# Streaming the weights instead of the activations in two weight-heavy products of a two-block transformer kernel

## The chip, the cores and the metric

The kernel runs on one core of a Trainium2 chip. The metric is device time in microseconds (us) for one execution. The program is one launch; the weights come from device memory in 404 blocks of 128 x 1024 float32 numbers (512 KB), used in a fixed order.

Names of the engines in the profile: PE is TensorE's matmul, PEld its load of a stationary operand, DVE is VectorE, ACT ScalarE, POOL GpSimd, SP the engine whose queue issues the block loads.

## The reference, cut to what matters

Two transformer blocks over 256 tokens of width 1024. The change touches one product of each:

```python
def chunk(xc):                                   # first block, expert layer, 16384 experts
    ...
    u_sel = jnp.take(u, experts, axis=0)
    act = gelu(einsum('cd,chkd->chk', xc, u_sel))
    v_sel = jnp.take(v, experts, axis=0)
    return einsum('chk,chkd->cd', (g * act), v_sel)

def conv_ffn(h, w_up, conv_w, conv_b, w_down):   # second block
    u = causal_dwconv(h @ w_up, conv_w, conv_b)
    a, g = jnp.split(u, 2, axis=-1)
    return (silu(a) * g) @ w_down                # w_down: 2752 x 1024
```

The kernel does not gather experts. It keeps a dense routing matrix G (tokens by experts), computes every expert's activation 128 experts at a time, multiplies by G, and multiplies by all rows of `v`: 128 products of (256 tokens x 128 experts) by (128 experts x 1024). The down projection is 22 such products. Each adds into the same 1024 x 256 sum.

## The kernel before, in words

**High and low parts.** A product in float32 precision is made of three in the format fp32r: high weights by high activations, high weights by low activations, low weights by high activations. For each block, ACT writes the high part `w_hi` (L588), then DVE (L1042) or POOL (L487) writes the low part `w_lo = raw - w_hi`. Between block 109 and the end, POOL owns the even blocks (and block 109), DVE the odd ones (`lo_owner`). The rings `raw`, `w_hi`, `w_lo` have four places: ACT may convert block n when PE has finished block n-4 (semaphore `block_used`).

**Two kinds of block.** `project` (L1642) multiplies a block by 1024-wide tokens into one PSUM bank, 24 matmuls, 256 columns moving. `expand` (L2019) takes 128 activations per token from `h_op` (high and low part, two buffers) and adds a 1024 x 256 result into PSUM banks 4 to 7 over all calls, also 24 matmuls: the weight tile of 128 x 128 is stationary, the 256 tokens move. It is called 150 times.

**The stages that call it.** The order within each engine is written out by hand.

- V stage: 64 `expand` blocks in a row. For each, DVE multiplies the stored activation by G (L1383), casts the high part (L1390), subtracts for the low part (L1392; together `split`), and after every other one makes a `w_lo` (L1042). POOL makes the `w_lo` between.
- Chunk stage: 64 times `project` (next 128 experts), ACT's gelu (L888), `split`, `expand`. Per pair of blocks ACT converts two, POOL and DVE make one `w_lo` each.
- FFN stage: 22 tiles, each of two `project` (both halves of the up projection) and one `expand`. DVE adds the earlier token to the PSUM sum (L1565, twice), does four taps of the convolution (L1574) after ACT's first tap (L997), and the gate (L1585, L1590, L1592). Tiles alternate in how many `w_lo` fall to DVE and to POOL: three each in two tiles.

**After the last `expand`** of the V and chunk sum, `add_sum` (L1441) adds the four banks to the residual `res`, ACT and DVE make the operands of the next projection (L621, L1073), ACT squares `res` for the norm, and PE sums the squares (L1657). After the last `expand` of the FFN, the same add leads to the final norm and the output.

Of the kernel before, what the change touches and what calls it, by code (L numbers as in the profile page):

```python
# [29 lines left out]
ALU = mybir.AluOpType  # L30
ACT = mybir.ActivationFunctionType
AX = mybir.AxisListType

P = 128
D = 1024
KT = D // P
NQ = 256
# [23 lines left out]
FT = -(-FF // P)  # L61
# [10 lines left out]
B_IN2 = B_PEER + 2 * (NKEYS - EARLY)  # L72
# [4 lines left out]
N_BLOCKS = B_FFN + 3 * FT  # L77
# [58 lines left out]
def build(nc, dram):  # L136
    ctx = ExitStack()
    with ctx:
# [5 lines left out]
        def sem(name):  # L144
            if name not in sems:
                sems[name] = ctx.enter_context(nc.semaphore(name))
            return sems[name]
# [3 lines left out]
        w_hi = sb("w_hi", [P, RING, D], F32R)  # L151
        w_lo = sb("w_lo", [P, RING, D], F32R)
# [10 lines left out]
        h_op = sb("h_op", [P, 2, 2, NQ], F32R)  # L163
        big = sb("big", [P, NKEYS * NQ])

        ps = ctx.enter_context(nc.psum_tensor("ps", [P, 8, 512], F32))
# [15 lines left out]
        xf = area(KT * NK)  # L182
# [127 lines left out]
        ident = con("ident")  # L310
# [24 lines left out]
        M_IN2 = M_PEER  # L335
# [3 lines left out]
        M_FFN = M_XO + 2  # L339
# [43 lines left out]
        def outputs_read(o):  # L383

            return min(o - 1, HEADS) if o <= HEADS + DH else o - 1

        def walk(a, b):

# [192 lines left out]
        def _(act):  # L581
# [10 lines left out]
            def his(upto):  # L592
                while ahead[0] < min(upto, N_BLOCKS):
                    if lo_owner(ahead[0]):
                        hi(At(ahead[0]))
                    ahead[0] += 1
# [126 lines left out]
            for h in range(DH):  # L723
                for t in range(2):
                    start = FAR - N_META - P * t
# [181 lines left out]
            act.dma_start(w_gate, dram["w_gate"]).then_inc(sem("cst2_loaded"), 16)  # L907
            act.dma_start(flat2(kv_x), mem_store).then_inc(sem("kv_back"), 16)

            def residual_squares(r):  # L910

                for b in range(4):
                    act.wait_ge(sem("res_ready"), 4 * r + b + 1)
                    squares(flat2(res[:, 2 * b:2 * b + 2, :]), 2 * b, NQ, 2)

            his(B_IN2 + 2)
            act.wait_ge(sem("block_used"), B_IN2 - 2)
            for b in range(4):
                act.wait_ge(sem("res_ready"), b + 1)
# [18 lines left out]
            for n in range(NCH):  # L938
                last = csum[:, CHUNK * n + CHUNK - 1:CHUNK * n + CHUNK]
# [60 lines left out]
            def silu(p):  # L1000

                act.wait_ge(sem("conv_done"), p.value(2 * p.first + 1, 2 * p.stride))
                act.activation(act_a[:, p.mod(2), :], conv_a[:, p.mod(2), :], ACT.Silu).then_inc(sem("silu_done"), 1)
# [13 lines left out]
                    tile(At(1 + j, i, 4))  # L1017
            taps(At(FT - 1))
            silu(At(FT - 1))
            residual_squares(1)  # L1020
            root(R_FINAL, NQ)
            for f in range(2):
# [7 lines left out]
        def _(dve):  # L1030
# [401 lines left out]

            def add_sum(r):

                for b in range(4):
                    if b < 3:
                        dve.wait_ge(sem("sum_ready"), 3 * r + b + 1)
                    else:
                        dve.wait_ge(sem("block_used"), (B_IN2, N_BLOCKS)[r])
                    two = flat2(res[:, 2 * b:2 * b + 2, :])  # L1440
                    dve.tensor_tensor(two, ps[:, 4 + b, :], two, ALU.add).then_inc(sem("res_ready"), 1)  # L1441
                    if r == 0 and b:
                        gained_lo(R_MIX, "mix", range(2 * b - 2, 2 * b))

# [26 lines left out]
            for n in range(NCH):  # L1471
                c = slice(CHUNK * n, CHUNK * n + CHUNK)
# [46 lines left out]
            for t in range(2):  # L1519
                w = [pcol("scw", 3 * t + j) for j in range(3)]  # L1520
# [102 lines left out]
        def _(pe):  # L1623
            def parts(s, wa, wb, k_hi, k_lo):

                return ((w_hi[:, s, wa:wb], k_hi), (w_hi[:, s, wa:wb], k_lo), (w_lo[:, s, wa:wb], k_hi))
# [34 lines left out]
            def norm(r, T, bank=2):  # L1661
                for k in range(KT):
                    norm_sum(r, k, T, bank)
# [116 lines left out]
            for h in range(HEADS):  # L1780
                mm = pe.matmul(ps[0:8, 3, 0:NK], one_in[0:NOPE, 7 - h:15 - h], sq[0:NOPE, h * NK:(h + 1) * NK],
                               start=False, stop=(h == HEADS - 1))
# [199 lines left out]
            last = B_BESIDE - B_EARLY - 1  # L1982
# [29 lines left out]
            def expand(n, b, first, last):  # L2012

                s = n.mod(RING)
                for k in range(KT):
                    out = ps[:, 4 + k // 2, (k % 2) * NQ:(k % 2 + 1) * NQ]
                    for j, (w, x) in enumerate(parts(s, P * k, P * k + P, h_op[:, b, 0, :], h_op[:, b, 1, :])):

                        mm = pe.matmul(out, w, x, start=(first and j == 0 and k % 2 == 0), stop=(last and j == 2),  # L2019
                                       skip_group_check=True)  # L2020
                    if last and k % 2 and k < KT - 1:
                        mm.then_inc(sem("sum_ready"), 1)
                mm.then_inc(sem("block_used"), 1)

            def early(c):
                n = At(B_V + c.first, c.i, c.stride)
# [26 lines left out]
            arrived(At(B_IN2 - 1))  # L2053
            pe.wait_ge(sem("acts_ready"), NKEYS)
            expand(At(B_IN2 - 1), (NKEYS - 1) % 2, False, True)

# [125 lines left out]
            def down(p, n, last=False):  # L2184
                arrived(n)
                pe.wait_ge(sem("acts_ready"), p.value(NKEYS + p.first + 1))
                expand(n, p.mod(2), p.first == 0, last)
# [8 lines left out]
            with pe.Fori(0, (FT - 2) // 4) as i:  # L2196
                for j in range(4):
                    tile(At(1 + j, i, 4))
            down(At(FT - 1), At(N_BLOCKS - 1), last=True)
            norm(R_FINAL, NQ)  # L2200


# [138 lines left out]
```

## Time and profile before

| | |
|---|---|
| median of 3 runs | 1556.12 us (1554.26 to 1560.02) |
| profiled execution, first to last instruction (span) | 1548.2 us |
| median less span: start and end around it | 7.9 us |
| PE busy | 1435.7 us (93% of the span) |
| DVE busy | 1175.8 us (76%) |
| ACT busy | 684.5 us (44%) |
| POOL busy | 674.5 us (44%) |
| V stage | 592 to 788 us |
| chunk stage | 788 to 1153 us |
| FFN stage, steady part | 1366 to 1533 us |

The profiled execution has no time of its own beside its span, so the 7.9 us is the difference to the median of the runs. PE's busy share counts overlapping matmuls and does not say that PE is at its peak. An operation that waits for a resource which another engine holds is shown as busy for the whole time, so a long duration of a short operation is a wait.

### The profile page before, as it was taken

To read this page: it belongs to the slowest core of one execution; us is meant where nothing else is said; L and a number is where in the kernel's file an instruction comes from. 1 tells how busy PE (TensorE), PEld (TensorE's weight loads), DVE (VectorE), ACT (ScalarE), POOL (GpSimd) and SP (SyncE) were. 2 spreads that over 40 slices of the span, in tenths; PEclk is the share of its full clock that TensorE was granted. 3 is DMA by queue.
4 is the path that set the end of the run, shared out by engine and by line. 5 is a ranking of instruction groups with operands and counts; after the bars stand their busy time and mean duration, and the time that the engine had idled before them with its cause. 6 is when DMAs were issued, how large, how long until landed. Compare 5 with 4: busy or idle time off the path is not lost.

```text
span 1548.2 us, 31404 instructions
## 1 busy us (share of the span) xinstructions
PE 1435.7 (93%) x11038; PEld 1350.0 (87%) x11038; DVE 1175.8 (76%) x2036; ACT 684.5 (44%) x1035; POOL 674.5 (44%) x300
## 2 busy tenths in 40 slices
PE   7999898998688889899999999999999989899997
PEld 5776588998688889899999999999999968699997
DVE  4424637889899998888878888888875654499997
ACT  4434544444344443333334444444446346555553
POOL 2313246779444443433434444444433335255441
PEclk9999989999799999999999999999999999999999
DMA  7411045666333335666656655565563323255552
GB/s 277 130 55 41 28 139 188 186 196 178 119 116 113 108 114 169 214 213 213 218 169 188 188 179 181 184 189 183 184 211 119 127 96 112 79 183 184 189 176 81
DMA packets 79624, 240.69 MB, mean 155 GB/s; under 512 B 8896, under 2 KB 25552, under 8 KB 78928
## 3 DMA queue, kind: packets, MB, share of 16 engines
q1 hardware_dynamic: 75744, 228.75, 46.2%
q10 hardware_dynamic: 3824, 11.17, 2.0%
q8 instruction: 38, 0.62, 0.2%
q14 instruction: 18, 0.15, 0.0%
HBM read 229.37 MB, written 10.52 MB: 155 GB/s over the span
## 4 chain that ended last, share of the span: by engine, by line
PE 68%; DVE 25%; issue 3%; ACT 1%; DVEq 1%; DMA 0%; POOL 0%; ACTq 0%
PE ps L1642 36%; PE ps L2019 20%; DVE work L1364 6%; DVE work L1383 3%; DVE work L1365 2%; DVE h_op L1390 2%; DVE w_lo L1042 2%; PE ps L1906 2%; PE ps L1860 1%; DVE h_op L1392 1%; PE ps L1657 1%; DVE big L1351 1%; PE ps L1831 1%; DVE big L1349 1%; PE ps L1880 1%
## 5 line engine op out<-in xcount | busy, mean ns | idle before, releaser
L487 POOL TENSOR_TENSOR w_lo<-raw,w_hi 128x1024 fp32r<-128x1024 f32 x241 | 622.0, 2583 | 748.6 <-ACT w_hi L588 748.6
L1642 PE MATMUL ps<-x_op,w_hi 128*128 128x256 f32 (+1 forms) x3968 | 746.7, 289 | 21.1 <-DVE x_op L1060 8.8
L1642 PEld LDWEIGHTS ps<-x_op,w_hi 128*128 128x128 f32 x3968 | 627.8, 194 | 34.3 <-issue 21.2
L1642 PE MATMUL ps<-x_op,w_lo 128*128 128x256 f32 (+1 forms) x1984 | 567.5, 286 | 0.0
L588 ACT ACTIVATE w_hi<-raw 128x1024 fp32r<-128x1024 f32 x400 | 420.5, 1055 | 270.0 <-PE ps L2019 218.2
L2019 PE MATMUL ps<-h_op,w_hi 128*128 128x256 f32 x2400 | 429.3, 280 | 17.1 <-DVE h_op L1392 14.7
L1642 PEld LDWEIGHTS ps<-x_op,w_lo 128*128 128x128 f32 x1984 | 385.7, 194 | 0.0
L2019 PEld LDWEIGHTS ps<-h_op,w_hi 128*128 128x128 f32 x2400 | 367.0, 188 | 19.8 <-DVE h_op L1392 13.6
L2019 PE MATMUL ps<-h_op,w_lo 128*128 128x256 f32 x1200 | 336.2, 280 | 0.0
L1042 DVE TENSOR_TENSOR w_lo<-raw,w_hi 128x1024 fp32r<-128x1024 f32 x159 | 203.7, 1281 | 39.5 <-ACT w_hi L588 39.3
L2019 PEld LDWEIGHTS ps<-h_op,w_lo 128*128 128x128 f32 x1200 | 225.3, 188 | 0.0
L1392 DVE TENSOR_TENSOR h_op<-work,h_op 128x256 fp32r<-128x256 f32 x128 | 194.3, 1518 | 4.4
L1383 DVE TENSOR_TENSOR work<-work,big 128x256 f32<-128x256 f32 x124 | 99.8, 805 | 66.0 <-ACT work L888 65.0
L1364 DVE TENSOR_SCALAR work<-kept,route_t 128x128 f32<-128x128 f32 x256 | 132.8, 519 | 4.7 <-PE ps L2002 2.6
L2002 PE MATMUL ps<-work 128*128 128x128 f32 x512 | 71.2, 283 | 29.3 <-DVE work L1365 29.3
L1365 DVE TENSOR_SCALAR work<-kept,route_t 128x128 f32<-128x128 f32 x256 | 95.4, 373 | 0.0
L2002 PEld LDWEIGHTS ps<-work 128*128 128x128 f32 x512 | 62.9, 193 | 35.2 <-DVE work L1365 35.2
L888 ACT ACTIVATE work<-ps 128x256 f32<-128x256 f32 x64 | 24.7, 386 | 125.0 <-PE ps L1642 125.0
L1390 DVE CAST h_op<-work 128x256 fp32r<-128x256 f32 x128 | 59.4, 464 | 25.7 <-PE ps L2019 14.6
L843 ACT ACTIVATE kv_mem<-ps 128x256 f32<-128x256 f32 x64 | 24.6, 384 | 96.3 <-PE ps L1642 96.3
L868 ACT ACTIVATE big<-ps 128x512 f32 (+1 forms) x64 | 38.2, 598 | 65.3 <-PE ps L2002 65.3
L524 POOL TENSOR_TENSOR big<-big 128x544 f32<-128x544 f32 (+1 forms) x24 | 25.6, 1068 | 81.5 <-DVE big L1229 81.5
(267 smaller groups left out, 1079.4 us busy)
## 6 DMA issues: line engine op xcount, KB each, us to landing
raw<-blocks SPq DMA_DIRECT2D x404, 512.0 KB, 3.4
early_store<-kv_mem SPq DMA_DIRECT2D x60, 128.0 KB, 3.2
work<-early_store SPq DMA_DIRECT2D x60, 128.0 KB, 3.3
big<-consts ACTq DMA_DIRECT2D x2, 1336.0 KB, 6.7
big<-h_t ACTq DMA_DIRECT2D x4, 272.0 KB, 3.9
big<-bias_lines ACTq DMA_DIRECT2D x8, 136.0 KB, 2.6
bias_lines<-route_t ACTq DMA_DIRECT2D x4, 264.0 KB, 3.0
res<-mem_t SPq DMA_DIRECT2D x1, 1024.0 KB, 9.2
```

The source lines that it names most:

```text
L487: pool.tensor_tensor(w_lo[:, s, :], raw[:, s, :], w_hi[:, s, :].bitcast(F32), ALU.subtract).then_inc(sem("lo_pool"), 1)
L588: act.activation(w_hi[:, s, :], raw[:, s, :], ACT.Copy).then_inc(sem("hi_done"), 1)
L868: act.activation(big[:, bass.ds(At(512 * g, i, 4096).value(), 512)], ps[:, 2 + g % 2, :], ACT.Copy).then_inc(sem("g_ready"), 1)
L1042: dve.tensor_tensor(w_lo[:, s, :], raw[:, s, :], w_hi[:, s, :].bitcast(F32), ALU.subtract).then_inc(sem("lo_dve"), 1)
L1364: dve.tensor_scalar(one1[:, g, j, :], con("iota"), route_t[:, 0, tok], None, ALU.is_equal)
L1365: return dve.tensor_scalar(one2[:, g, j, :], con("iota"), route_t[:, 1, tok], route_t[:, 2, tok], ALU.is_equal, ALU.mult)
L1383: dve.tensor_tensor(hf[:, b, :], a, G[:, :, bass.ds(chunk.value(), 1)].rearrange("p t e -> p (t e)"), ALU.mult).then_inc(sem("act_used"), 1)
L1390: dve.tensor_copy(h_op[:, b, 0, :], hf[:, b, :]).then_inc(sem("act_hi"), 1)
L1392: dve.tensor_tensor(h_op[:, b, 1, :], hf[:, b, :], h_op[:, b, 0, :].bitcast(F32), ALU.subtract).then_inc(sem("acts_ready"), 1)
L1642: mm = pe.matmul(ps[:, m_bank, 0:T], w, x, start=(k == 0 and j == 0), stop=(k == last and j == 2))
L2002: mm = pe.matmul(ps[:, 2 + g % 2, P * k:P * k + P], one1[:, g % 2, k, :], one2[:, g % 2, k, :], start=True, stop=True)
L2019: mm = pe.matmul(out, w, x, start=(first and j == 0 and k % 2 == 0), stop=(last and j == 2), skip_group_check=True)
```

## The change: activations stationary, weights moving

In `expand` the roles are exchanged. A tile of activations (128 inner values x 128 tokens) is stationary, and 512 columns of the weight block move. Twelve matmuls of 512 columns take the place of 24 of 256. The sum in banks 4 to 7 now stands with tokens on the partitions, so at the end of each of the two sums it is copied to SBUF (banks in the order of `SUM_ORDER`, ACT the first and third, DVE the second and fourth), transposed by PE in 16 steps into banks 3, 0, 4 and 6, and added to `res` from there.

```diff
+        SUM_ORDER = ((0, 0), (1, 0), (0, 1), (1, 1))
+        sums = xf[:, 0:4 * 512].rearrange("p (j c) -> p j c", j=4)
+        def sum_bank(t, f):
+            return 4 + 2 * t + f
+        def turned_bank(b):
+            return (3, 0, 4, 6)[b]
...
+            def copy_sum(r):
+                for j in (0, 2):
+                    act.wait_ge(*sum_done(r, j))
+                    act.activation(sums[:, j, :], ps[:, sum_bank(*SUM_ORDER[j]), :], ACT.Copy).then_inc(sem("sum_copied_act"), 1)
...
             def add_sum(r):
+                for j in (1, 3):
+                    dve.wait_ge(*sum_done(r, j))
+                    dve.tensor_copy(sums[:, j, :], ps[:, sum_bank(*SUM_ORDER[j]), :]).then_inc(sem("sum_copied_dve"), 1)
                 for b in range(4):
-                    if b < 3:
-                        dve.wait_ge(sem("sum_ready"), 3 * r + b + 1)
-                    else:
-                        dve.wait_ge(sem("block_used"), (B_IN2, N_BLOCKS)[r])
+                    dve.wait_ge(sem("sum_turned"), 4 * r + b + 1)
...
             def expand(n, b, first, last):
                 s = n.mod(RING)
-                for k in range(KT):
-                    out = ps[:, 4 + k // 2, (k % 2) * NQ:(k % 2 + 1) * NQ]
-                    for j, (w, x) in enumerate(parts(s, P * k, P * k + P, h_op[:, b, 0, :], h_op[:, b, 1, :])):
-                        mm = pe.matmul(out, w, x, start=(first and j == 0 and k % 2 == 0), stop=(last and j == 2),
+                for j, (t, f) in enumerate(SUM_ORDER):
+                    out, c = ps[:, sum_bank(t, f), :], slice(P * t, P * t + P)
+                    high, low = h_op[:, b, 0, c], h_op[:, b, 1, c]
+                    w_high, w_low = w_hi[:, s, 512 * f:512 * f + 512], w_lo[:, s, 512 * f:512 * f + 512]
+                    pe.matmul(out, high, w_high, start=first, stop=False)
+                    pe.matmul(out, high, w_low, start=False, stop=False)
+                    mm = pe.matmul(out, low, w_high, start=False, stop=last)
...
+            def turn_sum(r):
+                if r == 1:
+                    pe.wait_ge(sem("bank_free"), M_FFN + 2 * FT)
+                for j, (t, f) in enumerate(SUM_ORDER):
+                    pe.wait_ge(sem("sum_copied_act" if j % 2 == 0 else "sum_copied_dve"), 2 * r + j // 2 + 1)
+                    for k in range(4):
+                        mm = pe.transpose(ps[:, turned_bank(2 * f + k // 2), (k % 2) * NQ + P * t:(k % 2) * NQ + P * t + P],
+                                          sums[:, j, P * k:P * k + P], ident)
+                        if t and k % 2:
+                            mm.then_inc(sem("sum_turned"), 1)
```

On PE, the beginning of one `expand` in the V stage, before. The names are output, moving operand, stationary operand; a row's count is of equal instructions in a row, and `acts_ready` is what `split` signals.

```order
L2019 MATMUL ps<-h_op,w_hi 128x256 [waits acts_ready,lo_pool]
L2019 MATMUL ps<-h_op,w_hi 128x256
L2019 MATMUL ps<-h_op,w_lo 128x256
L2019 MATMUL ps<-h_op,w_hi 128x256 x2
L2019 MATMUL ps<-h_op,w_lo 128x256
```

The same place in the changed kernel:

```order
L2044 MATMUL ps<-w_hi,h_op 128x512 [waits acts_ready,lo_pool]
L2045 MATMUL ps<-w_lo,h_op 128x512
L2046 MATMUL ps<-w_hi,h_op 128x512
L2044 MATMUL ps<-w_hi,h_op 128x512
L2045 MATMUL ps<-w_lo,h_op 128x512
```

The waits stay at the same place; eight such groups of three become four, each of twice the columns.

On PE, from the end of the last `expand` of the V and chunk sum to the next projection (L1642 before, L1667 in the changed kernel), before:

```order
L2019 MATMUL ps<-h_op,w_hi 128x256 x2
L2019 MATMUL ps<-h_op,w_lo 128x256
L1642 MATMUL ps<-x_op,w_hi 128x256 [waits x_even,bank_free,lo_dve]
L1642 MATMUL ps<-x_op,w_hi 128x256
L1642 MATMUL ps<-x_op,w_lo 128x256
```

and in the changed kernel:

```order
L2046 MATMUL ps<-w_hi,h_op 128x512
L2058 MATMUL ps<-kept,big 128x128 [waits sum_copied_act]
L2058 MATMUL ps<-kept,big 128x128 x3
L2058 MATMUL ps<-kept,big 128x128 [waits sum_copied_dve]
L2058 MATMUL ps<-kept,big 128x128 x3
L2058 MATMUL ps<-kept,big 128x128 [waits sum_copied_act]
L2058 MATMUL ps<-kept,big 128x128 x3
L2058 MATMUL ps<-kept,big 128x128 [waits sum_copied_dve]
L2058 MATMUL ps<-kept,big 128x128 x3
L1667 MATMUL ps<-x_op,w_hi 128x256 [waits x_even,bank_free,lo_dve]
```

Sixteen transposes with four waits on copies now stand between the sum and the projection; at the end of the FFN they stand ahead of the final norm's sums.

On DVE, the same place, before (L1042 is the `w_lo` of an odd block, L1073 the low part of the next operand):

```order
L1042 TENSOR_TENSOR w_lo<-raw,w_hi 128x1024 [waits hi_done]
L1441 TENSOR_TENSOR res<-ps,res 128x512 [waits sum_ready] x2
L1073 SCALAR_TENSOR_TENSOR x_op<-res,par,x_op 128x256 [waits rms_hi] x2
L1441 TENSOR_TENSOR res<-ps,res 128x512 [waits sum_ready]
L1073 SCALAR_TENSOR_TENSOR x_op<-res,par,x_op 128x256 [waits rms_hi] x2
```

and in the changed kernel:

```order
L1067 TENSOR_TENSOR w_lo<-raw,w_hi 128x1024 [waits hi_done]
L1462 COPY big<-ps 128x512 [waits sum_ready]
L1462 COPY big<-ps 128x512 [waits block_used]
L1466 TENSOR_TENSOR res<-ps,res 128x512 [waits sum_turned] x2
L1098 SCALAR_TENSOR_TENSOR x_op<-res,par,x_op 128x256 [waits rms_hi] x2
```

Two copies come ahead of the first add, and the second copy waits for the whole sum. Between these places the order of ACT, DVE, POOL and SP is unchanged.

## Rows read from the trace of the kernel before

**Rows 1.** The page: the span.

```profile
span 1548.2 us, 31404 instructions
```

**Rows 2.** Windows by stage: length, busy of PE, PEld, DVE, ACT, POOL; clock, DMA.

```profile
592.00:788.00 196.00, 182.72 (x1537) 180.72 (x1537) 169.09 (x222) 68.33 (x65) 80.39 (x32) 1.00 0.65 208
788.00:1153.00 365.00, 363.62 (x3059) 363.44 (x3058) 291.35 (x255) 150.12 (x189) 153.60 (x63) 1.00 0.59 183
...
1366.00:1533.00 167.00, 166.14 (x1393) 165.97 (x1393) 150.83 (x209) 87.25 (x116) 77.99 (x28) 1.00 0.51 170
```

**Rows 3.** Chain that ended last, chunk stage: start, length, what.

```profile
870.09 2.83 PE ps L2019 x24
...
875.80 2.83 PE ps L2019 x24
```

**Rows 4.** Timeline of DVE, chunk stage: start, length, what, [idle before].

```profile
876.43 0.64 DVE L1383 TENSOR_TENSOR work<-work,big 128x256 f32<-128x256 f32 x1 [0.94 <-ACT work L888]
```

**Rows 5.** Timelines of DVE and POOL, V stage.

```profile
649.05 2.46 POOL L487 TENSOR_TENSOR w_lo<-raw,w_hi 128x1024 fp32r<-128x1024 f32 x1 [2.97 <-ACT w_hi L588]
...
649.33 2.67 DVE L1383 TENSOR_TENSOR work<-work,big 128x256 f32<-128x256 f32 x1
...
652.79 1.22 DVE L1042 TENSOR_TENSOR w_lo<-raw,w_hi 128x1024 fp32r<-128x1024 f32 x1
...
658.97 1.22 DVE L1042 TENSOR_TENSOR w_lo<-raw,w_hi 128x1024 fp32r<-128x1024 f32 x1
...
661.96 2.62 POOL L487 TENSOR_TENSOR w_lo<-raw,w_hi 128x1024 fp32r<-128x1024 f32 x1 [4.92 <-ACT w_hi L588]
...
663.62 1.11 DVE L1390 CAST h_op<-work 128x256 fp32r<-128x256 f32 x1 [1.31 <-PE ps L2019]
```

**Rows 6.** Chain, memory keys: float32 matmuls of 256 columns, stationary 128 x 128.

```profile
140.43 3.46 PE ps L1831 x16
```

**Rows 7.** Timeline of PE: one-column matmuls, and 128 x 128 transposes.

```profile
98.98 1.84 PE L1791 MATMUL ps<-ones,big 96*128 96x1 f32 x16
...
1213.73 1.04 PE L2120 MATMUL ps<-kept,big 128*128 128x128 f32 x8
```

**Rows 8.** Chain, FFN stage.

```profile
1365.90 3.09 PE ps L2019 x24
1368.99 5.74 PE ps L1642 x48
```

**Rows 9.** Timelines of ACT, POOL and DVE, FFN stage.

```profile
1365.42 0.43 DVE L1592 TENSOR_TENSOR h_op<-work,h_op 128x256 fp32r<-128x256 f32 x1
...
1371.89 1.06 ACT L588 ACTIVATE w_hi<-raw 128x1024 fp32r<-128x1024 f32 x1 [1.26 <-PE ps L1642]
...
1373.03 3.49 POOL L487 TENSOR_TENSOR w_lo<-raw,w_hi 128x1024 fp32r<-128x1024 f32 x1 [1.08 <-ACT w_hi L588]
...
1373.03 1.22 DVE L1042 TENSOR_TENSOR w_lo<-raw,w_hi 128x1024 fp32r<-128x1024 f32 x1
1374.17 0.42 DVE L1565 TENSOR_TENSOR big<-ps,big 128x256 f32<-128x256 f32 x1
...
1375.58 2.88 DVE L1574 SCALAR_TENSOR_TENSOR big<-big,par 128x255 f32<-128x255 f32 x4 [0.38 <-ACT big L997]
...
1382.50 0.43 DVE L1592 TENSOR_TENSOR h_op<-work,h_op 128x256 fp32r<-128x256 f32 x1
1384.64 2.13 DVE L1574 SCALAR_TENSOR_TENSOR big<-big,par 128x255 f32<-128x255 f32 x4
```

**Rows 10.** Timelines of DVE and PE at the two ends.

```profile
1155.27 1.28 DVE L1441 TENSOR_TENSOR res<-ps,res 128x512 f32<-128x512 f32 x2
1156.59 1.65 DVE L1073 SCALAR_TENSOR_TENSOR x_op<-res,par,x_op 128x256 fp32r<-128x256 f32 x2
...
1535.86 3.62 PE L1657 MATMUL ps<-big,ones 128*128 128x256 f32 x16
```

**Rows 11.** Groups by line: a copy of 128 x 512 from PSUM on DVE.

```profile
L1504 DVE COPY big<-ps 128x512 f32<-128x512 f32 x2 | 1.3, 688 | 0.0
```

More of the change, by code:

```diff
@@ L385, in outputs_read, with sum_done @@
             return min(o - 1, HEADS) if o <= HEADS + DH else o - 1
+        SUM_ORDER = ((0, 0), (1, 0), (0, 1), (1, 1))
[4 more added lines that the diff above has]
+            return (3, 0, 4, 6)[b]
+        assert M_IN2 % 2 == 1
+        def sum_done(r, j):
+            return (sem("sum_ready"), 3 * r + j + 1) if j < 3 else (sem("block_used"), (B_IN2, N_BLOCKS)[r])
         def walk(a, b):
@@ L916, in _ @@
             his(B_IN2 + 2)
+            copy_sum(0)
             act.wait_ge(sem("block_used"), B_IN2 - 2)
@@ L1019, in _ @@
             silu(At(FT - 1))
+            copy_sum(1)
             residual_squares(1)
@@ L1433, in add_sum @@
             def add_sum(r):
+                for j in (1, 3):
+                    dve.wait_ge(*sum_done(r, j))
+                    dve.tensor_copy(sums[:, j, :], ps[:, sum_bank(*SUM_ORDER[j]), :]).then_inc(sem("sum_copied_dve"), 1)
                 for b in range(4):
-                    if b < 3:
-                        dve.wait_ge(sem("sum_ready"), 3 * r + b + 1)
-                    else:
-                        dve.wait_ge(sem("block_used"), (B_IN2, N_BLOCKS)[r])
+                    dve.wait_ge(sem("sum_turned"), 4 * r + b + 1)
                     two = flat2(res[:, 2 * b:2 * b + 2, :])
-                    dve.tensor_tensor(two, ps[:, 4 + b, :], two, ALU.add).then_inc(sem("res_ready"), 1)
+                    dve.tensor_tensor(two, ps[:, turned_bank(b), :], two, ALU.add).then_inc(sem("res_ready"), 1)
                     if r == 0 and b:
@@ L2014, in expand @@
                 s = n.mod(RING)
-                for k in range(KT):
-                    out = ps[:, 4 + k // 2, (k % 2) * NQ:(k % 2 + 1) * NQ]
-                    for j, (w, x) in enumerate(parts(s, P * k, P * k + P, h_op[:, b, 0, :], h_op[:, b, 1, :])):
-                        mm = pe.matmul(out, w, x, start=(first and j == 0 and k % 2 == 0), stop=(last and j == 2),
-                                       skip_group_check=True)
-                    if last and k % 2 and k < KT - 1:
+                for j, (t, f) in enumerate(SUM_ORDER):
[5 more added lines that the diff above has]
+                    mm = pe.matmul(out, low, w_high, start=False, stop=last)
+                    if last and j < 3:
                         mm.then_inc(sem("sum_ready"), 1)
                 mm.then_inc(sem("block_used"), 1)
+            def turn_sum(r):
[8 more added lines that the diff above has]
+                            mm.then_inc(sem("sum_turned"), 1)
             def early(c):
@@ L2055, in _ @@
             expand(At(B_IN2 - 1), (NKEYS - 1) % 2, False, True)
+            turn_sum(0)
             def project_in2(j, count=1):
@@ L2199, in _ @@
             down(At(FT - 1), At(N_BLOCKS - 1), last=True)
+            turn_sum(1)
             norm(R_FINAL, NQ)
```

## The prediction, made before the changed kernel was run

> **What bounds the kernel now.** I read the windows by stage first, then the chain of waits, then the timelines of DVE and POOL beside it, because the windows alone mislead. They show PE busy in 363.62 of 365 us in the chunk stage, in 166.14 of 167 us in the FFN stage, and in 182.72 of 196 us in the V stage, all at the full granted clock of 1.00 (2.4 GHz) [rows 2]. So PE bounds the first two and something else takes 13.3 us in the third.
>
> The chain gives PE's unit: one `expand` takes 2.83 us, or 118 ns for each of its 24 matmuls, and in the chunk stage one comes every 5.71 us without a gap (from 870.09 to 875.80) [rows 3]. DVE has a reserve of 0.94 us in each such pair, which is its wait for ACT's gelu [rows 4].
>
> In the V stage the reader is to look at DVE and POOL together. POOL's `w_lo` takes 2.46 us from 649.05; a DVE multiply that begins at 649.33 takes 2.67 us, and ends about half a microsecond after POOL [rows 5]. An ordinary one takes 0.62 (0.64 in the chunk stage [rows 4]), so the POOL operation cost DVE 2.05 us. The Trainium skill (SBUF — State Buffer, "Who interferes with whom") says that such operations on the two engines exclude each other through a shared pair of ports; the trace agrees with its 2.67 us. DVE's round of two blocks, from `w_lo` to `w_lo`, is 6.18 us (652.79 to 658.97) [rows 5]. Two `expand` need only 5.66. The stage's average is 196/32 = 6.13 us for two blocks [rows 2]. DVE's waits for PE are no reserve: the one ahead of 663.62 lies inside the POOL operation from 661.96, which would have blocked the cast anyway [rows 5]. DVE and POOL bound the V stage.
>
> **The price of a 512-column matmul.** None in the trace has the form fp32r with 512 columns. The nearest rows are float32 matmuls with a 128 x 128 stationary tile and 256 columns, which count twice in the records and stream 512 column times each: 16 in 3.46 us, 216.3 ns each [rows 6]. Matmuls that move a single column still take 1.84/16 = 115 ns each, the last one's latency included [rows 7]. That is the loading of a stationary tile. It is about as long as the streaming of 256 columns (107 ns at 2.4 GHz) and would explain why these cost 118; behind 512 columns (213 ns) it disappears. I take 216.3: twelve are 2.60 us, 0.235 less than now. The bound below is pure streaming, 2.56 us (0.27 less). The bound above is that all of the 118 ns goes with the columns, 236 ns each, and nothing is gained.
>
> A rule speaks against the change. The Trainium skill (TensorE: Matmul & The Clock Gate, "Back-to-back issue gap") gives columns/2.4 + 2.5 ns for a matmul. By it an `expand` would cost 24 x 109.2 = 2.62 us now and 12 x 215.8 = 2.59 us then, so only 0.03 us would be saved. The 2.83 us of the trace contradicts its first half.
>
> **Part by part.**
>
> Chunk stage: the first 62 `expand` stand on the chain, 62 x 0.235 = 14.6 us less. The new period of 5.47 leaves DVE 0.94 - 0.24 = 0.70 us of reserve. POOL's operation there follows ACT's gelu, so its place against DVE does not move.
>
> V stage: PE could run two blocks in 5.19 us but gets its operands every 6.18. All waits now fall to PE, and DVE runs in its fully blocked round: 32 x (6.18 - 6.13) = 1.6 us more. The bounds are the cost of a POOL operation to DVE, 2.05 us or its whole 2.46 us, and a round as short as 6.0: -4 to +12 us.
>
> FFN stage: this decides. PE's period for two tiles is 2 x (5.74 + 2.83) = 17.14 to 17.17 us [rows 3, 8]. DVE's own, from the gate of tile 1 to that of tile 3, is 17.08 (1365.42 to 1382.50) [rows 9]. So a faster `expand` can gain 0.09 us in two tiles, not 0.47; from there PE waits for `acts_ready`. And then the order of two requests changes. In the even tile ACT converts a block when PE's `project` has ended (1371.89), and POOL asks for the ports at 1373.03. At this moment DVE begins its own `w_lo` (L1042, 1373.03). DVE was first: its operation takes the ordinary 1.22 us and POOL's takes 3.49 [rows 9]. POOL then works while DVE adds from PSUM (L1565, ordinary 0.42 us at 1374.17) and waits for PE and ACT, so only the first tap is late: four taps from 1375.58 take 2.88 us where 2.13 is ordinary, as if begun at 1376.33 [rows 9]. That tile is the one in which PE waited for DVE: `expand` began at 1365.90, just after the gate's end at 1365.85 [rows 8, 9]. This is the state in which PE will always be. With `expand` 0.235 shorter, POOL asks at 1372.8, while DVE is still in the L1592 ahead (0.43 us long, as at 1365.42 [rows 9]), and L1042 comes behind POOL. L1042 and the adds are then late by about 2.25 us (between the 2.05 above and POOL's 2.46). The first add comes at 1376.4, and the taps follow it by 1.41 as now (1374.17 to 1375.58), at 1377.8 instead of 1376.33: 1.4 us more of a DVE round. The round becomes 18.5 us against PE's 17.17. Nine whole rounds lie between tile 1 and tile 19: 9 x 1.33 = 12 us more. Since PE waits for DVE again at the next odd tile, the order cannot right itself. The bounds are a gain of 9 x 0.09 = 0.8 us if DVE stays first, and 14 us.
>
> End of the first sum: ACT and DVE are late there now, not PE (the first add begins at 1155.27, directly behind a `w_lo` [rows 10]). The gains of the last two `expand` are hidden by that. DVE's two copies cost 0.69 us each [rows 11]. They push the adds by 1.4 us. But the two operations behind the adds take 1.65 us today, from 1156.59 [rows 10], and I count about half of that as a wait for POOL, which will be over by then. I take 0.4 us. Sixteen transposes (eight take 1.04 us [rows 7]) run behind the copies. Bounds 0 to 2.
>
> End of the second sum: now the adds run beside the last `expand`, and the final sums of squares start at once (1535.86, 16 in 3.62 us [rows 10]). Then `expand` ends 0.23 earlier, PE turns eight tiles (1.04 us [rows 7]) before the first add can start, and add (0.69) and square (0.6) follow: the sums start at 1537.7, 1.8 us later. If the pause brings the clock to its lower level, these matmuls double: bounds 1.3 to 5.4.
>
> Sum: -14.6 + 1.6 + 12 + 0.4 + 1.8 = +1.2 us. The profiled span of 1548.2 [rows 1] becomes 1549.4; with the 7.9 us around it, the median of 1556.1 becomes 1557.3.
>
> **The rivals.**
>
> 1. DVE stays first in the FFN stage, because its next instruction is queued closely enough behind L1592 to win. Against it, POOL asks 0.2 us ahead in my reckoning; for it, the trace shows nearly a tie. Then -14.6 + 1.6 - 0.8 + 0.4 + 1.8 = -11.6 us: 1544.5 us.
> 2. The DVE round isn't a fixed quantity, and a PE that is never late shortens it in the V stage too: half of 64 x 0.235 there, so -11.6 - 7.5 - 1.6: about 1535 us. PE's 13 us of waits in that stage speak against it.
> 3. The change does not shorten a matmul (236 ns for 512 columns). Then only the ends remain: 1558 us.
> 4. Slower: in the V stage each POOL operation costs DVE its full 2.46 us and PE's requests come where DVE is never at rest. The round becomes 6.5 us, 32 x 0.37 = 12 us more instead of 1.6: 1568 us. It decides from a round of 6.34 us on, since 32 x 0.21 = 6.6 us reach the limit of 1563.9. The blocked 2.05 us measured today speaks against it.
>
> **How the numbers follow.** My forecast has a chance of 0.40, rival 1 of 0.25, rival 2 of 0.12, rival 3 of 0.08, rival 4 of 0.15. The likeliest time is 1557. The range goes from below rival 1 (with 0.27 instead of 0.235 for an `expand`, 1542, and something of rival 2) to rival 4: 1540 to 1567. The forecast's own range is 1550 to 1563, from chunk gains of 11 to 17 us and an FFN loss of 8 to 14. A measurement tells about 0.5% (7.8 us) from no change. Faster by more than that (under 1548.3): nearly all of rivals 1 and 2 and the lowest edge of the forecast, 0.38. Slower (over 1563.9): most of rival 4 and the upper edge of the forecast, 0.16. Within: 0.46.
>
> **What the new profile would show.** PE starts of the 512-column matmuls 216 ns apart and an `expand` of 2.60 us; a chunk period of 5.47 us; V rounds of 6.18 us with PE idle near 1 us in each; in even FFN tiles, a `w_lo` on DVE of over 3 us and a POOL one of 2.5 instead of 3.49, and DVE rounds of 18.5 us. I am wrong at the largest term if those DVE rounds stay at 17.1, and at the first one if the period in the chunk stage is not 5.47.

## The result, and the profile after

The changed kernel takes 1568.43 us (median of 6 runs, 1561.96 to 1574.15) against 1557.05 us for the kernel before on the same chip (6 runs, 1554.09 to 1561.39). The ratio is 1.0073 (95% interval 1.0043 to 1.0102), so it is slower by 0.7%, or 11.4 us. I had forecast 1557, within a range of 1540 to 1567, with a chance of 0.16 for slower. The result is just outside the range.

Not all executions of a kernel are alike: the lower TensorE's mean granted clock in one, the longer it takes. Three of the six above had a clock of 0.969 to 0.972 and took 1570.14 to 1574.15 us, the other three 0.975 or 0.976 and 1561.96 to 1566.71. The kernel before, in 25 later runs, shows the same: fifteen at 0.963 to 0.972 with a median of 1561.0 us, ten at 0.974 to 0.976 with 1554.6. Like beside like, the changed kernel is 11.5 and 10.7 us slower, so the clock does not make the difference.

The page of the changed kernel: its span, the chain by engine, and one group (line, engine, operation, count | busy us, mean ns | idle before it and its releaser).

```profile
span 1570.6 us, 27877 instructions
...
PE 57%; DVE 33%; issue 6%; ACT 2%; DVEq 2%; ACTq 0%; DMA 0%; POOL 0%
...
L2044 PE MATMUL ps<-w_hi,h_op 128*128 128x512 f32 x600 | 240.1, 400 | 30.3 <-DVE h_op L1417 16.3
```

DVE now makes up 33% of the chain that ended last, where it was 25%. The profiled execution took 1572.5 us, 1.9 more than its span. In the prediction I had put 7.9 us around the span of before. Every run since is 1.8 to 2.0 us longer than its span, so some 6 of the 7.9 us were no start or end, but a profiled execution quicker than the median (clock 0.976).

The same windows as in [rows 2], with the two ends added:

```profile
592.00:788.00 196.00, 181.07 (x766) 142.56 (x766) 172.80 (x222) 68.32 (x65) 79.52 (x32) 1.00 0.65 209
788.00:1153.00 365.00, 363.62 (x2311) 328.45 (x2309) 292.17 (x255) 152.20 (x192) 153.63 (x64) 1.00 0.59 185
1153.00:1180.00 27.00, 24.03 (x177) 22.41 (x177) 17.26 (x34) 20.72 (x39) 8.11 (x3) 1.00 0.44 157
1366.00:1533.00 167.00, 156.00 (x1081) 144.48 (x1080) 153.18 (x189) 78.52 (x108) 71.03 (x28) 1.00 0.51 169
1533.00:1570.00 37.00, 26.27 (x166) 23.00 (x164) 26.75 (x44) 14.74 (x22) 5.41 (x2) 0.94 0.19 71
```

In the chunk stage PE is as busy as before, 363.62 of 365 us. In the FFN stage it was busy in 166.14 of 167 us and is now busy in 156.00.

**Chunk stage.** The chain (start, length, what), with the places of [rows 3]: one `project` follows another every 5.65 us, and twelve matmuls stand between them.

```profile
873.24 2.86 PE ps L1667 x24
876.10 0.23 PE ps L2044
876.33 0.23 PE ps L2045
876.57 0.23 PE ps L2046
...
878.65 0.23 PE ps L2046
878.89 2.86 PE ps L1667 x24
```

From 876.10 to 878.89 an `expand` takes 2.79 us, 232.5 ns for each matmul of 512 columns. Before, it took 2.83 [rows 3]. The period falls from 5.71 to 5.65 us, not to 5.47, and the stage takes 3.3 us less.

**V stage.** DVE's timeline, as in [rows 5]:

```profile
646.59 1.22 DVE L1067 TENSOR_TENSOR w_lo<-raw,w_hi 128x1024 fp32r<-128x1024 f32 x1
...
649.30 2.67 DVE L1408 TENSOR_TENSOR work<-work,big 128x256 f32<-128x256 f32 x1
...
652.76 1.22 DVE L1067 TENSOR_TENSOR w_lo<-raw,w_hi 128x1024 fp32r<-128x1024 f32 x1
```

The round is 6.17 us, and the stage, which begins at 592.3 us in both kernels, ends (with the first `project` of the next) at 789.60 instead of 788.54: 1.1 us later.

**FFN stage.** Timelines of ACT, POOL and DVE, with the gates of tiles 1 to 3 (L1617), to be laid beside [rows 9]:

```profile
1372.63 0.43 DVE L1617 TENSOR_TENSOR h_op<-work,h_op 128x256 fp32r<-128x256 f32 x1
...
1379.07 1.06 ACT L605 ACTIVATE w_hi<-raw 128x1024 fp32r<-128x1024 f32 x1 [1.22 <-PE ps L1667]
1379.90 0.43 DVE L1617 TENSOR_TENSOR h_op<-work,h_op 128x256 fp32r<-128x256 f32 x1
1380.21 2.39 POOL L504 TENSOR_TENSOR w_lo<-raw,w_hi 128x1024 fp32r<-128x1024 f32 x1 [1.04 <-ACT w_hi L605]
1380.24 3.44 DVE L1067 TENSOR_TENSOR w_lo<-raw,w_hi 128x1024 fp32r<-128x1024 f32 x1
1383.60 0.74 DVE L1590 TENSOR_TENSOR big<-ps,big 128x256 f32<-128x256 f32 x2
1385.01 2.14 DVE L1599 SCALAR_TENSOR_TENSOR big<-big,par 128x255 f32<-128x255 f32 x4 [0.67 <-ACT big L1021]
...
1391.19 0.43 DVE L1617 TENSOR_TENSOR h_op<-work,h_op 128x256 fp32r<-128x256 f32 x1
```

Before, both `w_lo` began at 1373.03, and the 3.49 us fell to POOL and the 1.22 to DVE [rows 9]. Now POOL begins 0.03 us ahead and takes 2.39, and DVE's operation takes 3.44. The adds, the taps and the gate all come behind it. The round from gate to gate is 18.56 us (1372.63 to 1391.19) where it was 17.08 [rows 9]. From the gate of tile 1 to that of tile 21 it is 179.87 us, where it was 166.99 (from the gate at 1365.42 [rows 9] to the one at 1532.41): 12.9 us more.

The shortest lead that POOL has over DVE in the nine even tiles 2 to 18 is 0.03 us, and DVE's operation takes 3.42 to 3.44 us in all nine. In the kernel before, the tie exists only in tile 2. PE's two tiles take 17.18 us there (1374.73 to 1391.91) and DVE's 17.08, so PE, and with it POOL, falls behind: at tile 18 DVE begins at 1509.71 and POOL at 1510.41. In the changed kernel PE waits for DVE's gate at the odd tiles again and again (1.23 us ahead of the `expand` at 1391.67), and so the two meet each time as in tile 2.

**The ends.** From the end of the last `project` of the chunk stage (1147.29, before 1149.56) to the next norm's sums (1160.53, before 1162.99) it is 13.24 us, where it was 13.43: 0.2 us less. Two effects are added up in this. To the first matmul of the next projection (1156.18, before 1157.99) it is 8.89 us instead of 8.43, 0.5 more. From there to the sums it is 4.35 instead of 5.00, because before, the granted clock was at its lower level for a part of it (mean 0.59 from 1160 to 1163 us, after PE had been idle for 2.61 us ahead of the projection). In the changed kernel the transposes stand in this gap, the longest idle time is 0.90 us, and the clock stays at 1.00. The end of the second sum, PE and DVE:

```profile
1552.50 0.43 DVE L1617 TENSOR_TENSOR h_op<-work,h_op 128x256 fp32r<-128x256 f32 x1
...
1555.95 1.91 PE L2058 MATMUL ps<-kept,big 128*128 128x128 f32 x16
...
1556.81 2.48 DVE L1466 TENSOR_TENSOR res<-ps,res 128x512 f32<-128x512 f32 x4
```

From this gate to the end of the span it is 18.15 us, before 15.75 (1532.41 to 1548.16): 2.4 us more.

Together: -3.3 (62 x 0.053, chunk stage) + 1.1 (V) + 12.9 (FFN) - 0.2 and + 2.4 (ends) = +12.9 us. The medians show +11.4, with an interval of +6.7 to +15.9.

The span differs by 22.4 us, so some 10 us lie elsewhere. They are in the attention stretch between the two blocks, which the change doesn't touch. One window of it in the changed kernel, and the same in the kernel before:

```profile
1260.00:1280.00 20.00, 20.00 (x50) 10.63 (x49) 8.53 (x21) 7.81 (x24) 4.16 (x4) 0.50 0.00 0
```

```profile
1260.00:1280.00 20.00, 19.31 (x82) 11.25 (x82) 10.76 (x27) 12.54 (x38) 6.72 (x7) 0.88 0.00 1
```

The granted clock is 0.50 there, the lower level of 1.2 GHz, against a mean of 0.88. From 1160 to 1340 us it is 0.88 against 0.94. In the profile of the FFN-only variant below, it is 0.94 in that stretch again. So I count the 10 us to the execution, which is one of the three at the lower clock, beside a profile of before at 0.976. The comparison of like with like above has no room for 10 us more.

### The profile page after: what moved, and what is told of

Read it like the earlier page. It is cut to its first block, busy times and chain, and to the rows that moved or that the text cites. A ratio compares the mean times of both kernels' runs of the same rounds, so it can differ in the third digit from the quotient of the medians.

```text
span 1570.6 us, 27877 instructions
## 1 busy us (share of the span) xinstructions
PE 1445.7 (92%) x9270; PEld 1269.1 (81%) x9270; DVE 1194.7 (76%) x2040; ACT 683.4 (44%) x1039; POOL 668.6 (43%) x300
## 4 chain that ended last, share of the span: by engine, by line
PE 57%; DVE 33%; issue 6%; ACT 2%; DVEq 2%; ACTq 0%; DMA 0%; POOL 0%
PE ps L1667 29%; DVE work L1389 6%; PE ps L2044 5%; PE ps L2045 5%; PE ps L2046 5%; DVE w_lo L1067 4%; DVE work L1610 3%; DVE work L1408 3%; DVE work L1390 2%; DVE h_op L1415 2%; PE ps L1931 2%; DVE big L1599 2%; PE ps L1885 2%; DVE h_op L1417 1%; PE ps L1682 1%
## 5 line engine op out<-in xcount | busy, mean ns | idle before, releaser
L1667 PE MATMUL ps<-x_op,w_hi 128*128 128x256 f32 (+1 forms) x3968 | 744.4, 289 | 19.4 <-DVE x_op L1085 8.8
L1667 PEld LDWEIGHTS ps<-x_op,w_hi 128*128 128x128 f32 x3968 | 631.2, 194 | 40.2 <-issue 19.0
L1667 PE MATMUL ps<-x_op,w_lo 128*128 128x256 f32 (+1 forms) x1984 | 566.1, 285 | 0.0
L1667 PEld LDWEIGHTS ps<-x_op,w_lo 128*128 128x128 f32 x1984 | 384.0, 194 | 0.0
L2044 PE MATMUL ps<-w_hi,h_op 128*128 128x512 f32 x600 | 240.1, 400 | 30.3 <-DVE h_op L1417 16.3
L1067 DVE TENSOR_TENSOR w_lo<-raw,w_hi 128x1024 fp32r<-128x1024 f32 x159 | 224.1, 1409 | 36.8 <-ACT w_hi L605 36.7
L2045 PE MATMUL ps<-w_lo,h_op 128*128 128x512 f32 x600 | 237.0, 395 | 0.0
L2046 PE MATMUL ps<-w_hi,h_op 128*128 128x512 f32 x600 | 236.6, 394 | 0.0
L2044 PEld LDWEIGHTS ps<-w_hi,h_op 128*128 128x128 f32 x600 | 112.9, 188 | 60.7 <-DVE h_op L1417 17.8
L2046 PEld LDWEIGHTS ps<-w_hi,h_op 128*128 128x128 f32 x600 | 112.8, 188 | 27.4
L2045 PEld LDWEIGHTS ps<-w_lo,h_op 128*128 128x128 f32 x600 | 112.7, 188 | 22.2
```

The source lines that it names most:

```text
L1067: dve.tensor_tensor(w_lo[:, s, :], raw[:, s, :], w_hi[:, s, :].bitcast(F32), ALU.subtract).then_inc(sem("lo_dve"), 1)
L1667: mm = pe.matmul(ps[:, m_bank, 0:T], w, x, start=(k == 0 and j == 0), stop=(k == last and j == 2))
L2044: pe.matmul(out, high, w_high, start=first, stop=False)
L2045: pe.matmul(out, high, w_low, start=False, stop=False)
L2046: mm = pe.matmul(out, low, w_high, start=False, stop=last)
```

## The experiments

The price of the 512-column matmul and the order at the ports were the two disputed steps. The first experiment measures the price by itself. The next two apply the change in one place each. Two more force the order of the requests, once each way. The last two take POOL out of the contest.

### e1_price: the matmul by itself

A kernel that only issues rows of 48 independent matmuls of one form each:

```diff
+            for i in range(COUNT):
+                mm = pe.matmul(ps[:, i % 4, 0:512], s_r[:, i % 2, :], m_r[:, 0:512], start=True, stop=True)
+            for i in range(COUNT):
+                mm = pe.matmul(ps[:, i % 4, 0:256], s_r[:, i % 2, :], m_r[:, 0:256], start=True, stop=True)
+            for i in range(COUNT):
+                mm = pe.matmul(ps[0:32, i % 4, 0:512], s_r[:, i % 2, 0:32], m_r[:, 0:512], start=True, stop=True)
...
```

> A kernel of its own that computes nothing of the reference: it only runs rows of 48 matmuls back to back and reads their spacing. Forms, in order: fp32r with 512 columns moving and 128 stationary columns (twice, the first to bring the clock up), fp32r 256 columns, fp32r 512 and 256 columns with only 32 stationary columns, fp32r 384 columns, bf16 512 and 256, float32 512 and 256 (24 each). Theory 'columns': the moving operand of format fp32r takes about 0.454 ns per column, whatever is stationary: 232, 116, 232, 116 and 174 ns; bf16 comes near 216 and 109. Theory 'loading' (the one of the prediction): with 32 stationary columns the spacing falls to 216 and 109 ns, and with 128 it stays at 118 for 256 columns. If bf16 with 512 columns takes 232 too, neither the format nor the load is the cause.

PE's timeline (start, length of the whole row, form; `m_r` is fp32r, `m_b` bf16, `m_f` float32; 128*32 has a stationary tile of 32 columns):

```profile
21.28 11.04 PE L53 MATMUL ps<-m_r,s_r 128*128 128x512 f32 x48
32.16 5.91 PE L55 MATMUL ps<-m_r,s_r 128*128 128x256 f32 x48
37.91 11.28 PE L57 MATMUL ps<-m_r,s_r 128*32 128x512 f32 x48
49.02 5.62 PE L59 MATMUL ps<-m_r,s_r 128*32 128x256 f32 x48
54.48 8.49 PE L61 MATMUL ps<-m_r,s_r 128*128 128x384 f32 x48
62.81 10.53 PE L63 MATMUL ps<-m_b,s_b 128*128 128x512 bf16 x48
73.18 5.40 PE L65 MATMUL ps<-m_b,s_b 128*128 128x256 bf16 x48
78.42 20.77 PE L67 MATMUL ps<-m_f,s_f 128*128 128x512 f32 x48
99.03 10.52 PE L69 MATMUL ps<-m_f,s_f 128*128 128x256 f32 x48
```

I read a form's price from start to start: 227 ns for fp32r with 512 columns ((32.16 - 21.28)/48), 120 with 256, 173 with 384. With 32 stationary columns it is 231 ns (512) and 114 (256). In bf16 it is 216 and 109. The float32 matmuls have 48 records for 24 instructions, and a record of 512 columns takes 429 ns ((99.03 - 78.42)/48), so it streams 512 columns twice, 215 ns each.

Three things follow. The rows from which I took 216.3 ns [rows 6] were right for float32, but fp32r is another form and takes 11 ns more than bf16 at either length. My picture of a loading that disappears behind 512 columns is refuted: the surplus over pure streaming (213 and 107 ns) is 13 to 14 ns at both lengths. In the kernel it even grows, from 11 (118) to 19 (232.5), which is close to the other theory, a surplus that goes with the columns. A stationary tile of 32 columns does not bring the predicted 216 and 109 ns either. Last, halving the number of matmuls saves 2 x 120 - 227 = 13 ns for each pair here, and 2 x 118 - 232.5 = 3.5 ns in the kernel. I had counted on 20.

The rule of the Trainium skill (TensorE: Matmul & The Clock Gate, "Back-to-back issue gap"), which I set aside, gives 215.8 and 109.2 ns. The Trainium skill calls this, in the same section, the gap of an isolated matmul and has about 131 ns for 512 columns in a sustained stream, which no row here comes near. The trace agrees with the 215.8 and 109.2 for bf16 (216 and 109), but not for fp32r (227 and 120). What I had worked out from the rule, 0.03 us saved for an `expand`, came close to the 0.04 of the kernel, but by luck: in the kernel its two prices are 9 and 17 ns too low.

### e2_v_new: the new form in the V and chunk stages alone

```diff
-                expand(n, p.mod(2), p.first == 0, last)
+                expand_old(n, p.mod(2), p.first == 0, last)
...
-            turn_sum(1)
```

> The new form in the V and chunk stages alone; the FFN stage keeps the old matmuls and the old add. Theory 'order of requests in the FFN stage': the whole loss is gone, chunk stage 62 x 0.05 us faster, V stage +1: about 3 us faster than before, 1554; FFN rounds 17.1 to 17.2 us. Rival 'the ends' (copies and transposes): still some 5 us slower than before.

It took 1555.73 us (12 runs), against 1559.56 for the kernel before (25 runs). The ratio is 0.998 (0.9958 to 1.0002). By the stages, -3.3 + 1.1 - 0.2 = -2.4 us was to come, and the medians show 3.8 less. A gain near 14 us (0.991) is excluded; no gain at all is not.

The FFN round from tile 1 is 17.09 us (gates at 1363.87 and 1380.96), but not every one is. POOL's and DVE's `w_lo` of tiles 2, 4 and 6:

```profile
1371.48 3.50 POOL L504 TENSOR_TENSOR w_lo<-raw,w_hi 128x1024 fp32r<-128x1024 f32 x1 [1.07 <-ACT w_hi L605]
1371.49 1.22 DVE L1066 TENSOR_TENSOR w_lo<-raw,w_hi 128x1024 fp32r<-128x1024 f32 x1
...
1388.66 2.39 POOL L504 TENSOR_TENSOR w_lo<-raw,w_hi 128x1024 fp32r<-128x1024 f32 x1 [1.02 <-ACT w_hi L605]
1388.71 3.42 DVE L1066 TENSOR_TENSOR w_lo<-raw,w_hi 128x1024 fp32r<-128x1024 f32 x1
...
1407.28 3.51 POOL L504 TENSOR_TENSOR w_lo<-raw,w_hi 128x1024 fp32r<-128x1024 f32 x1 [1.06 <-ACT w_hi L605]
1407.29 1.22 DVE L1066 TENSOR_TENSOR w_lo<-raw,w_hi 128x1024 fp32r<-128x1024 f32 x1
```

In tile 4 the order changed, with the old matmuls, and the round from tile 3 took 18.71 us. DVE had begun the first add behind the gate of tile 3 0.13 us later than in the other odd tiles; what kept it, the trace does not say. (The changed kernel has the same delay there, and POOL's lead in tile 4 is 0.17 us.) One round later the order was as before, and it stayed so. With POOL 0.01 us ahead DVE's operation still took 1.22 us, twice; with POOL 0.05 us ahead it took 3.42. In the changed kernel POOL is never less than 0.03 us ahead. So in this round the old `expand` leaves the order just on the one side, and the one that is 0.04 us shorter puts it on the other.

### e3_ffn_new: the new form in the FFN alone

```diff
-                expand(n, c.mod(2), c.first == 0, False)
+                expand_old(n, c.mod(2), c.first == 0, False)
...
-            turn_sum(0)
```

> The new form in the FFN stage alone. Theory 'order of requests': DVE rounds of 18.6 us where 17.1 are needed, +13 us, and +2 for the end: about 1572. Rival 'the loss comes from the first stages or from a clock at its lower level between them': about 1559.

It took 1570.13 us (8 runs) against the same 1559.56, ratio 1.008 (1.0049 to 1.0111). POOL's and DVE's timelines show the place of [rows 9]:

```profile
1392.04 2.39 POOL L504 TENSOR_TENSOR w_lo<-raw,w_hi 128x1024 fp32r<-128x1024 f32 x1 [1.04 <-ACT w_hi L605]
```

```profile
1384.46 0.42 DVE L1628 TENSOR_TENSOR h_op<-work,h_op 128x256 fp32r<-128x256 f32 x1
...
1392.08 3.44 DVE L1066 TENSOR_TENSOR w_lo<-raw,w_hi 128x1024 fp32r<-128x1024 f32 x1
...
1403.05 0.43 DVE L1628 TENSOR_TENSOR h_op<-work,h_op 128x256 fp32r<-128x256 f32 x1
```

The round is 18.59 us and tile 1 to tile 21 takes 179.75. The gates before show 17.08 and 166.99. So the whole loss is made in the FFN: 12.8 us from gate to gate, where each `expand` is 0.04 us shorter and the order of the two requests has changed, and 2.4 us behind the last gate (18.16 us to the end of the span, before 15.75).

### e4_dve_first: the changed kernel, POOL made to ask second

POOL's `w_lo` of every third even block in the FFN waits until DVE has made the one of the block before:

```diff
-            even(B_FFN + 2, N_BLOCKS)
+            for n in range(B_FFN + 2, N_BLOCKS, 2):
+                if (n - B_FFN) % 6 == 0:
+                    pool.wait_ge(*rest_taken(At(n - 1)))
+                lo(At(n))
```

> The changed kernel, in which POOL in the FFN stage starts the low part of blocks 344, 350, ... only when DVE has made the one of the block before. Theory 'order of requests': L1067 takes its ordinary 1.22 us again, DVE rounds go back to 17.1 us, and the time to that of before, 1555 to 1557 (13 us under the changed kernel). Rival 'PE's shorter matmuls starve DVE or lack operands': rounds stay above 18, time stays at 1568.

It took 1558.06 us (12 runs), ratio to the kernel before 1.000 (0.9975 to 1.0024). The timelines of POOL and DVE:

```profile
1377.27 2.40 POOL L504 TENSOR_TENSOR w_lo<-raw,w_hi 128x1024 fp32r<-128x1024 f32 x1 [2.38 <-DVE w_lo L1070]
```

```profile
1375.97 1.22 DVE L1070 TENSOR_TENSOR w_lo<-raw,w_hi 128x1024 fp32r<-128x1024 f32 x1
...
1378.53 3.09 DVE L1602 SCALAR_TENSOR_TENSOR big<-big,par 128x255 f32<-128x255 f32 x4 [0.42 <-ACT big L1024]
...
1385.66 0.43 DVE L1620 TENSOR_TENSOR h_op<-work,h_op 128x256 fp32r<-128x256 f32 x1
```

DVE's `w_lo` is back at 1.22 us and the round is 17.3 us (1368.36 to 1385.66), where 17.1 was expected. From the gate of tile 1 to that of tile 21 it is 168.40 us, so 11.5 of the 12.9 us are gone. With all of the change in it, turning one order back takes the loss away. POOL's operation costs DVE about 1 us instead (3.09 for four taps of 2.13), as in the kernel before (2.88 [rows 9]).

### e5_pool_first: the kernel before, DVE made to ask second

The opposite case. Nothing of the change is in this kernel, and only DVE's `w_lo` behind the even gates waits for POOL's next one, nine times:

```diff
                 if n.plus(2).mod(2):
+                    if p.first not in (0, FT - 2):
+                        dve.wait_ge(*rest_taken(n.plus(3)))
                     lo(n.plus(2))
```

> The kernel before, old matmuls everywhere, with one wait added: in the even FFN tiles 2 to 18 DVE begins its low part L1042 behind the gate only when POOL has made the one of the block after it. That is the order that the changed kernel falls into. Theory 'order of requests': the nine rounds take 18.5 us instead of 17.1 to 17.2, 12 us more than before (about 1571), with no 512-column matmul in the program. Rival 'the new matmuls themselves cost the FFN stage its time': about 1559.

It took 1567.79 us (6 runs) against 1556.4 (11 runs), ratio 1.0078 (1.0051 to 1.0104). DVE's timeline:

```profile
1378.39 1.23 DVE L1042 TENSOR_TENSOR w_lo<-raw,w_hi 128x1024 fp32r<-128x1024 f32 x1 [2.43 <-POOL w_lo L487]
...
1387.12 0.42 DVE L1592 TENSOR_TENSOR h_op<-work,h_op 128x256 fp32r<-128x256 f32 x1
```

The waiting time is now shown as idle (2.43 us) and not as a long operation. The round is 18.85 us (1368.27 to 1387.12), 0.3 more than in the changed kernel, since here DVE waits for the semaphore behind POOL's operation. The order alone, without a single new matmul, costs the FFN 14.5 us from gate to gate (181.49), and the kernel 11.4 by the medians, as much as the whole change.

### e6_before_dve and e7_after_dve: every `w_lo` of the three stages on DVE

One POOL operation costs DVE 2.05 us or more, and the same operation on DVE costs it 1.14 (1.22 less the overlap with its neighbour). So in these two kernels, of before and of the change, DVE makes all of them:

```diff
 def lo_owner(n):
+    if B_V < n < B_IN2 or n >= B_FFN + 2:
+        return "dve"
     return "pool" if B_QUERY <= n <= B_V or n % 2 == 0 else "dve"
...
-            even(B_FFN + 2, N_BLOCKS)
...
+                lo(At(B_PEER + 3 + 2 * d))
                 lo(At(B_PEER + 4 + 2 * d))
```

POOL's loops over the even blocks go, and DVE gets a `lo` for each of them, beside the one of the odd block.

> The kernel before, with all low parts of the V, chunk and FFN blocks made by DVE and none by POOL. Theory 'ports': a POOL low part costs DVE 2.05 us or more, one of its own 1.14, so the V round falls from 6.13 us to PE's 5.6 (64 x 0.23 = 15 us less) and PE bounds all three stages: 1543. Rival 'DVE is bound by its own work': V rounds stay at 6 us, and nothing is gained or something lost.

> The changed kernel, with all low parts of the V, chunk and FFN blocks made by DVE. By the theory PE bounds everywhere, so each of about 148 expand gives its full 0.05 us (2.78 or 2.79 against 2.83), 7 us, less 2 us at the ends: 5 us under the same edit of the kernel before, about 1538. Rival 'the form gives nothing when PE bounds': the same time as that kernel.

The first took 1540.74 us (6 runs), ratio 0.9898 (0.9872 to 0.9923). The second took 1531.34 us (5 runs, 1528.25 to 1533.97), ratio 0.9839 (0.981 to 0.9867). It is the fastest kernel of the case, 25 us under the one before. The V stage in the windows, first without and then with the new form:

```profile
592.00:780.00 188.00, 188.00 (x1598) 188.00 (x1597) 160.40 (x258) 70.89 (x69) 0.00 (x0) 1.00 0.69 226
```

```profile
592.00:780.00 188.00, 188.00 (x845) 153.07 (x844) 161.25 (x261) 72.28 (x72) 0.00 (x0) 1.00 0.68 226
```

PE does not wait at all there, where it was idle for 13.3 us [rows 2]. The V stage takes 180.9 us in the first kernel (596.24 to 777.15), where it took 196.1: 15.2 of the 15.7 us gained are there. DVE's timeline in the second kernel shows the unblocked block:

```profile
642.18 1.23 DVE L1070 TENSOR_TENSOR w_lo<-raw,w_hi 128x1024 fp32r<-128x1024 f32 x1 [0.15 <-ACT w_hi L608]
...
644.98 1.23 DVE L1070 TENSOR_TENSOR w_lo<-raw,w_hi 128x1024 fp32r<-128x1024 f32 x1 [0.16 <-ACT w_hi L608]
```

A block takes 2.80 us (642.18 to 644.98), PE's own time for an `expand`, although DVE now makes every `w_lo`. In the FFN a tile takes 8.59 us in the first kernel and 8.53 in the second, which is 5.74 + 2.79. The medians differ by 9.4 us and the spans by 7.1 (1539.3 and 1532.2). Of these 7.1, 5.2 us are there at the last `split` of the chunk stage (1138.3 and 1133.1), 0.04 us for each `expand` so far. But not all of the rest comes from the change. From the first matmul of the next projection (1145.16 and 1140.42, 4.7 us apart) to the gate of tile 0 (1347.93 and 1339.44) 3.7 us are added, in the attention stretch that the change doesn't touch, at a granted clock of 0.92 against 0.94. The FFN from there to the last gate adds 1.0, and the end takes 2.4 back. So where PE bounds all three stages, the parts that the change touches gain some 3.3 us, 0.2%; 5 had been expected. The medians say 0.6%, but the six runs of the first kernel had a clock of 0.968 to 0.971 and the five of the second 0.972 to 0.978. Whether the change has a part in that, these runs do not show.

## Why the prediction was wrong, and what of it was right

**The price of a 512-column matmul: wrong, and nearly the whole miss.** The step that failed is "I take 216.3: twelve are 2.60 us, 0.235 less than now". They took 2.79 us, 0.04 us less. The chunk stage gained 3.3 us instead of 14.6. With -3.3 in its place, and all other terms as forecast, the sum would have been +12.5 us, against +12.9 by the stages and +11.4 by the medians. I had taken the price from a row of another number format, and had explained the 118 ns of the 256-column form by the loading of the stationary tile. That was an argument from the 115 ns of one-column matmuls [rows 7], and the first experiment refutes it: behind 512 columns the surplus is still there. The upper bound that I wrote down (236 ns) was close to the truth (232.5), and I gave it a chance of 0.08 only. Nor did I follow it through the sum: with 0 for the chunk stage and the other terms as they stood it gives +15.8 us, 1572, outside my range. The range ended even below the 1568 of my own rival 4. (The limit of that rival has a slip, too: to reach 1563.9 its V round has to be 6.39 us and not 6.34, since the 6.6 us come in addition to the 1.6 of the forecast.)

**Rival 3 had the price nearly right (236 ns for 232.5), and its time wrong.** I had worked it out as 1558, as if with an unchanged price nothing in the FFN could flip. But the tie there was so close (both requests at 1373.03 [rows 9]) that 0.04 us of PE was enough: POOL now asks at 1380.21 and DVE at 1380.24.

**FFN stage: right in mechanism and size, with luck.** 18.5 us was forecast for a round and 18.6 measured (18.7 in two of them); +12 us was forecast and +12.9 measured. A `w_lo` of 3.44 us on DVE and one of 2.39 on POOL are the two marks I had named. The FFN-only kernel shows that the loss is made here, and the two forced orders show that the order is its cause, once by taking the loss away and once by making it without the change. The luck is in the premise. I had POOL ask 0.2 us ahead, by an `expand` 0.235 us shorter. It asks 0.03 us ahead, and 0.01 us would not have been enough, as e2_v_new shows. So the term came true by some 0.02 us. Of "the order cannot right itself" the changed kernel is an example nine times over, but it is not so in general: with the old matmuls it righted itself after one round. Rival 1 (DVE stays first) is refuted for the change as it is; its round is what e4 shows.

**V stage: right.** 6.18 us forecast, 6.17 measured; +1.6 forecast, +1.1 measured. Only PE's idle time is less than I had said, about 0.5 us in a round (14.9 of 196 us) and not 1, because its matmuls are longer. Rival 2 (PE's speed shortens DVE's round) and rival 4 (a round of 6.5) are both refuted by that round. The last two experiments show what bounded it: without POOL's operations a block takes 2.80 us.

**The ends: right in size.** +0.4 was forecast for the first, and up to the next projection 0.5 was measured. The -0.2 that is left in sum comes from the clock, which no longer falls there; I had not thought of that. +1.8 was forecast and +2.4 measured for the second.

**Conversion to a median.** Taking the difference of median and span as a constant did no harm to the forecast of a difference. But the profile of one execution can be off by 10 us in a stretch that the change doesn't touch, so stages have to be compared one by one.

**What stays open.** Why fp32r with 512 columns takes 232.5 ns in the kernel but 227 by itself, while with 256 it takes 118 and 120. Why the clock is lower in some executions than in others, in every kernel here. What delayed DVE at tile 3 in e2_v_new.

## What to carry to other kernels

Take the price of an instruction from rows of its own format and size, and if there are none, let the forecast follow both bounds through every stage. Fewer and wider matmuls saved 1.5% of their time here, not 8%. Where two engines ask for one resource within hundredths of a microsecond of each other, a small change elsewhere decides who waits; ask whether the loser is the one on the chain, and follow the two over several rounds: here the tie of one tile became a lead of 0.70 us in the old kernel and stayed a tie in the new one. Work on a helping engine has to be weighed by what it takes from the engine that it helps: 2.05 us of blocking for 1.14 us of work was a loss, and giving it up gained 15.7 us. Compare executions at the same granted clock before giving a few microseconds to a change.

## What the runs showed of the hardware that was not expected

- An fp32r matmul takes longer than a bf16 one: 227 against 216 ns for 512 columns, 120 against 109 for 256, and 173 ns for 384. Each further column costs 0.42 ns in either form, so the difference is a fixed 11 ns for each matmul.
- A stationary tile of 32 columns instead of 128 changes the fp32r price by -6 ns with 256 columns and by +5 ns with 512.
- Two requests 0.03 us apart decide 2.2 us of blocking. POOL goes first when its `w_lo` begins 0.03 us or more ahead of DVE's (1380.21 and 1380.24 in the changed kernel); when it begins 0.01 us ahead, DVE goes first (1407.28 and 1407.29 in e2_v_new). POOL's operation takes 2.39 us when it is first and 3.49 us when DVE's is [rows 9].
- Sixteen 128 x 128 transposes in a gap of PE keep the clock up: without them it was idle for 2.61 us, and the granted clock fell to a mean of 0.59 from 1160 to 1163 us; with them it stayed at 1.00. The windows from 1153 to 1180 us show 0.94 in the three kernels whose first sum ends in the old way (before, e3_ffn_new, e5_pool_first) and 1.00 in the three with transposes there (changed, e2_v_new, e4_dve_first).
